# Products of high and low weight parts in the last two feed-forwards: three of 256 columns, or one of 512 and one of 256

## The reference, cut to what matters

```python
def swiglu(x, w_in, w_out):
    gate, up = jnp.split(x @ w_in, 2, axis=-1)
    return (jax.nn.silu(gate) * up) @ w_out
...
for layer in range(DEPTH):
    h = h + 0.5 * rmsnorm(swiglu(rmsnorm(h, g[0]), w_ffn_in[layer, 0], w_ffn_out[layer, 0]), g[1])
    ...  # the mixer, with its own norms
    h = h + 0.5 * rmsnorm(swiglu(rmsnorm(h, g[4]), w_ffn_in[layer, 1], w_ffn_out[layer, 1]), g[5])
```

## Time and profile before

| | |
|---|---|
| median of 3 runs | 1758.89 us (1758.84 to 1761.01) |
| profiled execution | 1760.43 us |
| its span, first to last instruction | 1758.4 us |
| TensorE busy (products) | 1723.0 us, 98% |
| TensorE weight loads busy | 1395.2 us, 79% |
| VectorE busy | 1053.0 us, 60% |
| ScalarE busy | 729.6 us, 41% |
| granted TensorE clock, mean | 0.995 of full |

### The profile page before, as it was taken

One profiled execution on the slowest core, in us unless ns is written; L12 is line 12 of the kernel. 1 busy time (PEld: TensorE's weight loads), 2 busy tenths in 40 slices (PEclk: granted clock), 3 DMA queues, 4 the chain that ended last, 5 costly groups with the idle time before them and its releaser, 6 DMA issues.

```text
span 1758.4 us, 31356 instructions
## 1 busy us (share of the span) xinstructions
PE 1723.0 (98%) x12314; PEld 1395.2 (79%) x12314; DVE 1053.0 (60%) x1905; ACT 729.6 (41%) x1191; POOL 21.2 (1%) x26
## 2 busy tenths in 40 slices
PE   9999999999999999999999999999999999999997
PEld 8999989899999999996899999998953333333332
DVE  7775475787765887578687657866762232222223
ACT  6444463464344544456754446957431101111110
POOL 0000000100000000000000001000020000000000
PEclk9999999999999999999999999999999999999999
DMA  6445334445454355432255545443889999999996
GB/s 243 189 171 193 138 121 161 65 147 191 175 203 149 143 192 203 182 121 95 96 182 200 204 178 193 145 147 119 331 340 428 428 426 428 427 429 428 428 426 258
DMA packets 42342, 409.73 MB, mean 233 GB/s; under 512 B 5304, under 2 KB 5304, under 8 KB 7056
## 3 DMA queue, kind: packets, MB, share of 16 engines
q1 hardware_dynamic: 40032, 402.21, 58.4%
q0 software_dynamic: 1936, 5.79, 1.6%
q10 hardware_dynamic: 288, 0.52, 0.1%
HBM read 405.87 MB, written 2.63 MB: 232 GB/s over the span
## 4 chain that ended last, share of the span: by engine, by line
PE 87%; DMA 6%; DVE 4%; ACT 2%; issue 1%; SPq 0%; DVEq 0%; ACTq 0%
PE ps L626 85%; PE ps L630 2%; DMA branch<-w_gate_up 2%; DMA late<-w_gate_up 2%; DMA soon<-w_gate_up 1%; DVE w_lo L1891 1%; DMA raw<-w_units 1%; ACT w_hi L1388 0%; DMA h<-xT 0%; DVE arena L2335 0%; DVE branch L1914 0%; DVE x_lo L1948 0%; DVE branch L1927 0%; DVE arena L2361 0%; DVE h L1938 0%
## 5 line engine op out<-in xcount | busy, mean ns | idle before, releaser
L626 PE MATMUL ps<-x_hi,w_hi 128*128 128x256 f32 (+1 forms) x2080 | 596.8, 287 | 3.9 <-DVE x_lo L1948 1.8
L626 PE MATMUL ps<-x_lo,w_hi 128*128 128x256 f32 (+1 forms) x2080 | 592.0, 285 | 0.0
L626 PE MATMUL ps<-x_hi,w_lo 128*128 128x256 f32 (+1 forms) x2080 | 590.4, 284 | 0.0
L1891 DVE TENSOR_TENSOR w_lo<-raw,w_hi 128x1024 fp32r<-128x1024 f32 (+1 forms) x352 | 448.2, 1293 | 129.8 <-ACT w_hi L1388 129.0
L1388 ACT ACTIVATE w_hi<-raw 128x1024 fp32r<-128x1024 f32 (+1 forms) x352 | 385.5, 1113 | 184.6 <-PE ps L626 102.1
L626 PEld LDWEIGHTS ps<-x_hi,w_hi 128*128 128x128 f32 x2080 | 391.2, 188 | 10.9 <-issue 6.9
L626 PEld LDWEIGHTS ps<-x_hi,w_lo 128*128 128x128 f32 x2080 | 393.1, 189 | 0.0
L626 PEld LDWEIGHTS ps<-x_lo,w_hi 128*128 128x128 f32 x2080 | 392.1, 189 | 0.3
L626 PE MATMUL ps<-hid_hi,w_hi 128*128 128x272 f32 (+1 forms) x704 | 200.9, 285 | 0.0
L626 PE MATMUL ps<-hid_hi,w_lo 128*128 128x272 f32 (+1 forms) x704 | 200.0, 284 | 0.0
L626 PE MATMUL ps<-hid_lo,w_hi 128*128 128x272 f32 (+1 forms) x704 | 199.4, 283 | 0.0
(11 more groups left out here) (345 smaller groups left out, 2095.4 us busy)
## 6 DMA issues: line engine op xcount, KB each, us to landing
raw<-w_units SPq DMA_DIRECT2D x144, 1024.0 KB, 4.8
soon<-w_gate_up SPq DMA_DIRECT2D x32, 2048.0 KB, 21.8
late<-w_gate_up SPq DMA_DIRECT2D x24, 2048.0 KB, 21.1
raw<-w_out_units SPq DMA_DIRECT2D x32, 1408.0 KB, 6.0
soon<-w_down SPq DMA_DIRECT2D x16, 2048.0 KB, 24.8
late<-w_down SPq DMA_DIRECT2D x12, 2048.0 KB, 22.2
branch<-w_gate_up SPq DMA_DIRECT2D x8, 2048.0 KB, 22.8
branch<-w_down SPq DMA_DIRECT2D x4, 2048.0 KB, 20.4
```

What stands on the lines that cost most here:

```text
L626: return nc.tensor.matmul(out_ap, lhsT, rhs, start=start, stop=stop, skip_group_check=True)
L1891: v.tensor_tensor(part(w_lo, c, 0, n), raw_slot(u, j * n, n), part(w_hi, c, 0, n).bitcast(F32), ALU.subtract).then_inc(lo_made, 1)
```

## The change

In feed-forwards 2 and 3, for units 2 to 21 inward and the first seven tiles outward, the products with the weights' high part become one: the high and low parts of the activations lie in one buffer with two planes (`x_both`, `hid_both`), and one product of 512 columns reads both and writes both halves of a bank. The product with the weights' low part adds into the first half. The two halves have to be added afterwards. Inward, ScalarE copies the second half to SBUF (`halves_copied`), VectorE adds the first half from PSUM, which frees the bank, and then scales (`halves_scaled`); the up tile's copy stands behind the gate's Silu on ScalarE. Outward, ScalarE copies the second half (`out_copied`), VectorE adds the first and frees the bank, and ScalarE squares and scales the sum (`out_scaled`). Buffer sizes don't change. Feed-forwards 0 and 1, units 0 and 1, the last outward tile and all other sections keep the three products.

```diff
+        x_both = sb("x_both", [P, 2, KT * TA], F32R)
+        x_hi, x_lo = x_both[:, 0, :], x_both[:, 1, :]
...
+        def pairs_before(n, it, j):
+            return 2 * ((FT - 2) * (n - 2) + j - 2) + 4 * it
...
+            def in_halves(bank, hi, lo, moving, start, stop):
+
+                first = mm(bank[:, 0:2 * SEQ].rearrange("p (a n) -> p a n", a=2), hi, moving, start, False)
+                return first, mm(bank[:, 0:SEQ], lo, moving[:, 0, :], False, stop)
...
+                        if both is not None:
+                            first, m = in_halves(bank, hi, lo, both[:, :, x], k == 0, k == kt - 1)
...
-                        project(u0 + j, T, 2 * j, X, w, it, 2 * RAW)
+                        project(u0 + j, T, 2 * j, X, w, it, 2 * RAW, both=x_both if w == SEQ else None)
...
+                        if w == SEQ and j < KT - 1:
+                            first, m = in_halves(bank, hi, lo, hid_both[:, :, x], k == 0, k == FT - 1)
...
+                    if halves and m < KT - 1:
+                        nc.scalar.activation(z, filled(t)[:, w:2 * w], ACT.Copy).then_inc(out_copied, 1)
+                        act.wait_ge(evac[t[0]], t[1] + 1)
+                        square(8 * (n // 2) + m, z, w)
+                        nc.scalar.activation(z, z, ACT.Copy, scale=gain(g, m, table)).then_inc(out_scaled, 1)
+                        continue
...
+                def gate_of_halves(j, it):
+                    tg, tu = T.at(2 * j, it, 4), T.at(2 * j + 1, it, 4)
+                    act.wait_ge(hw_made, FT * n + 2 * it + j - 1)
+                    act.wait_ge(full[tg[0]], tg[1] + 1)
+                    nc.scalar.activation(tile(sg, j, w), ps[tg[0]][:, w:2 * w], ACT.Copy).then_inc(halves_copied, 1)
+                    act.wait_ge(halves_scaled, pairs_before(n, it, j) + 1)
+                    nc.scalar.activation(tile(sg, j, w), tile(sg, j, w), ACT.Silu).then_inc(gate_silu, 1)
+                    act.wait_ge(hid_made, FT * n + 2 * it + j - 1)
+                    act.wait_ge(full[tu[0]], tu[1] + 1)
+                    nc.scalar.activation(tile(hw, j, w), ps[tu[0]][:, w:2 * w], ACT.Copy).then_inc(halves_copied, 1)
...
+                    if halves and m < KT - 1:
+                        t = T.at(m)
+                        z = tile(zg, m, w)
+                        copied[0] += 1
+                        dve.wait_ge(out_copied, copied[0])
+                        v.tensor_tensor(z, z, ps[t[0]][:, 0:w], ALU.add).then_inc(evac[t[0]], 1)
...
+                    elif w == SEQ and not (isinstance(it, int) and it == 0):
+                        c = pairs_before(n, it, j)
+                        dve.wait_ge(halves_copied, c + 1)
+                        v.tensor_tensor(g, g, ps[tg[0]][:, 0:w], ALU.add).then_inc(evac[tg[0]], 1)
+                        mine(tg)
+                        v.tensor_tensor(g, g, rs[:, 0:w], ALU.mult).then_inc(halves_scaled, 1)
+                        dve.wait_ge(halves_copied, c + 2)
+                        v.tensor_tensor(x, x, ps[tu[0]][:, 0:w], ALU.add).then_inc(evac[tu[0]], 1)
+                        mine(tu)
+                        v.tensor_tensor(x, x, rs[:, 0:w], ALU.mult).then_inc(halves_scaled, 1)
+                        dve.wait_ge(halves_scaled, c + 2)
```

More of the change, by code:

```diff
@@ L153, in two_blocks @@
         h = sb("h", [P, KT * TA])
-        x_hi = sb("x_hi", [P, KT * TA], F32R)
-        x_lo = sb("x_lo", [P, KT * TA], F32R)
+        x_both = sb("x_both", [P, 2, KT * TA], F32R)
+        x_hi, x_lo = x_both[:, 0, :], x_both[:, 1, :]
         branch = sb("branch", [P, (KT + 8) * TA])
@@ L178, in two_blocks @@
             with ExitStack() as ffn_only:
-                hid_hi = ffn_only.enter_context(nc.sbuf_tensor("hid_hi", [P, FT * TA], F32R))
-                hid_lo = ffn_only.enter_context(nc.sbuf_tensor("hid_lo", [P, FT * TA], F32R))
+                hid_both = ffn_only.enter_context(nc.sbuf_tensor("hid_both", [P, 2, FT * TA], F32R))
+                hid_hi, hid_lo = hid_both[:, 0, :], hid_both[:, 1, :]
                 ffn_only.enter_context(nc.sbuf_tensor("shared_keys", [P, 4 * TA], F32))
@@ L332, in two_blocks @@
         squared, sums_made = sem("squared"), sem("sums_made")
+        halves_copied, halves_scaled = sem("halves_copied"), sem("halves_scaled")
+        out_copied, out_scaled = sem("out_copied"), sem("out_scaled")
         route_sums = sem("route_sums")
@@ L670, in project @@
             def project(u, T, i, src, w, it=0, body=0, kt=KT, n_tiles=2, at=0, x_base=None, between=None, within=None,
-                        made=2, begun=0, done=0):
+                        made=2, begun=0, done=0, both=None):
                 if x_base is not None and n_tiles == 2:
@@ L688, in project @@
                             within()
-                        first, m = three(bank[:, 0:w], part(w_hi, c, a, P), part(w_lo, c, a, P),
-                                         src[0][:, x], src[1][:, x], k == 0, k == kt - 1)
+                        hi, lo = part(w_hi, c, a, P), part(w_lo, c, a, P)
+                        if both is not None:
+                            first, m = in_halves(bank, hi, lo, both[:, :, x], k == 0, k == kt - 1)
+                        else:
+                            first, m = three(bank[:, 0:w], hi, lo, src[0][:, x], src[1][:, x], k == 0, k == kt - 1)
                         if j % (n_tiles // 2) == 0 and k == 0:
@@ L779, in ffn @@
                         x = slice(k * TA, k * TA + w)
-                        first, m = three(bank[:, 0:w], part(w_hi, c, a, P), part(w_lo, c, a, P),
-                                         hid_hi[:, x], hid_lo[:, x], k == 0, k == FT - 1)
+                        hi, lo = part(w_hi, c, a, P), part(w_lo, c, a, P)
+                        if w == SEQ and j < KT - 1:
+                            first, m = in_halves(bank, hi, lo, hid_both[:, :, x], k == 0, k == FT - 1)
+                        else:
+                            first, m = three(bank[:, 0:w], hi, lo, hid_hi[:, x], hid_lo[:, x], k == 0, k == FT - 1)
                         if k % (FT // 2) == 0:
@@ L1447, in root_stat, with branch_out @@
                     nc.scalar.activation(std[:, 0:w], bank[:, 0:w], ACT.Sqrt, scale=1.0 / D).then_inc(evac[t[0]], 1)
-            def branch_out(name, n, g, table, w, per=2):
+            def branch_out(name, n, g, table, w, per=2, halves=False):
                 u0, T = plan[name]
@@ L1457, in branch_out @@
                     t = T.at(m)
+                    z = tile(zg, m, w)
[5 more added lines that the diff above has]
+                        continue
                     bank = filled(t)
                     square(8 * (n // 2) + m, bank[:, 0:w], w)
-                    nc.scalar.activation(tile(zg, m, w), bank[:, 0:w], ACT.Copy,
-                                         scale=gain(g, m, table)).then_inc(evac[t[0]], 1)
+                    nc.scalar.activation(z, bank[:, 0:w], ACT.Copy, scale=gain(g, m, table)).then_inc(evac[t[0]], 1)
                 root_stat(n, w)
@@ L1488, in gate @@
                     nc.scalar.activation(tile(sg, j, w), tile(sg, j, w), ACT.Silu).then_inc(gate_silu, 1)
+                def gate_of_halves(j, it):
[8 more added lines that the diff above has]
+                    nc.scalar.activation(tile(hw, j, w), ps[tu[0]][:, w:2 * w], ACT.Copy).then_inc(halves_copied, 1)
+                later_gate = gate_of_halves if w == SEQ else gate
                 if root is not None:
@@ L1501, in ffn @@
                             split_half(u0 + j + 2, 0, it)
-                            gate(j, it)
+                            later_gate(j, it)
                             split_half(u0 + j + 2, 1, it)
@@ L1507, in ffn @@
                 for j in range(2):
-                    gate(j, FT // 2 - 1)
+                    later_gate(j, FT // 2 - 1)
                     split_to(u0 + FT + j)
-                branch_out(f"out{n}", 2 * G_INDEX[n] + 1, g, halfg, w, 1)
+                branch_out(f"out{n}", 2 * G_INDEX[n] + 1, g, halfg, w, 1, w == SEQ)
             nc.scalar.preload_act_table(ACT.Square)
@@ L1861, in _ @@
         def _(dve):
-            chain, ahead, stds, highs, sums, turns = [0], [0], [0], [0], [0], [0]
+            chain, ahead, stds, highs, sums, turns, copied = [0], [0], [0], [0], [0], [0], [0]
             v = nc.vector
@@ L1973, in residual @@
                 u0, T = plan[name]
+                halves = per == 1 and w == SEQ
                 for m in range(KT):
                     split_to(u0 + m // per + 1, 2 if per == 1 else 2 + m % 2)
+                    if halves and m < KT - 1:
+                        t = T.at(m)
+                        z = tile(zg, m, w)
+                        copied[0] += 1
+                        dve.wait_ge(out_copied, copied[0])
+                        v.tensor_tensor(z, z, ps[t[0]][:, 0:w], ALU.add).then_inc(evac[t[0]], 1)
                     if m < KT - 1:
@@ L1988, in residual @@
                     mine(plan[f"stat{n}"].at(0))
```

(2 more changed lines are left out.)

## The result

The changed kernel takes 1791.92 us in the median (1789.86 to 1793.26, 4 runs) against 1759.72 (4 runs): ratio 1.0178, 95% interval 1.0166 to 1.0189, so 29 to 33 us slower. The forecast was 1791.5. The two profiled executions took 1760.43 and 1789.86 us, 29.4 apart, their spans 1758.4 and 1787.9.

What follows compares the result with a forecast made beforehand. TensorE was taken to bound the last two feed-forwards before, VectorE inward after the change. +35.7 us inward and -3.1 outward gave +32.6, 1793.0 us by the profile and 1791.5 against the median, range 1777 to 1809.

Steps and rivals of the forecast that it cites:

- The bound before: In the last two feed-forwards TensorE sets the pace, busy the whole 113.1 us; VectorE has about a fifth to spare.
- The unit of 6.43 us: Inward: VectorE's time for one changed unit, bounds 6.1 to 6.8, against 5.49 us of TensorE work.
- The sum inward, +35.7: Inward, both feed-forwards: TensorE starts its outward parts late by 19.8 and 15.9 us, +35.7 us.
- The outward sum, -3.1: Outward: 154 steps a feed-forward, each 10.2 ns shorter, 1.6 us twice, -3.1 us; ends 0 and -10.3.
- the 11.2 ns: TensorE's fixed part for each product whatever its width, beyond 106.7 ns for 256 columns at 2.4 GHz.
- The lower end, nothing saved: TensorE's step: the wide product costs as much as two halves made as two products, so nothing is saved.
- Rival (a): Inward: VectorE keeps up and TensorE is the bound again, 5.49 us a unit; with full gain 1749 us; chance 0.04.
- Rival (b): Inward: the weights' landing becomes the bound, 6.25 us a unit; with the longest landing 6.9, 1808 us; chance 0.12.
- Rival (d): Inward: TensorE's clock falls to 1.2 GHz from pausing each unit, a unit 10.8 us, +206 us; chance 0.02.
- The range: Whole kernel: 1777 to 1809 us, from 1779 to 1805 by the unit's bounds, widened by outward ends and the landing.
- the 7 us of the outward ends: Outward: what the ends of the gain there add to the range below; 3 us above.
- my 10.2: TensorE: ns saved by each changed step, 343.4 instead of 353.6, from taking the wide product at 225.5 ns.

Runs made afterwards that it cites:

- out_only: The changed kernel with only the outward part changed; inward keeps three products and the old evacuation: 1758.32 us, ratio 0.9994 to the kernel before.
- first_half: The changed kernel with wide products everywhere, but inward only the first half of the bank is read, with the old evacuation: 1756.51 us, ratio 0.9980.
- splits_first: The changed kernel with both second halves copied before Silu, both tiles added before scaling, and both weight splits ahead of the hidden part: 1758.44 us.
- in_only: The changed kernel with only the inward part changed; outward stays as before: 1792.31 us, ratio 1.0177 to the kernel before.
- chain_only: The changed kernel with each wide product made as two of 256 columns, keeping the new evacuation: 1794.58 us, ratio 1.0186 to the kernel before.
- early_up: The changed kernel with ScalarE copying the up tile's second half before Silu instead of behind it: 1768.25 us, ratio 1.0045 to the kernel before.

## Why the prediction was right

The direction, the place and the size came out by the mechanism forecast: VectorE's unit over TensorE's. Step by step:
- **The bound before**: right. out_only and first_half have TensorE busy throughout the stretch from 588 to 700 us.
- **The unit of 6.43 us**: 6.27 measured. The dependent step in the loop is 0.45 for the scalings (0.54 taken; only hid_lo has 0.56), the up addition comes at 1.63 instead of 1.74, the next split at 3.99 instead of 4.15. The step before hid_hi was 0.65 as taken. The splits' 2.28, for which no row was named, was met as well (661.95 - 659.67). The size was off by 2.5%, inside the bounds of 6.1 and 6.8.
- **The sum inward, +35.7**: from VectorE's first changed unit to outward, 120.2 and 117.5 us against 103.9 and 104.1, so +16.3 and +13.4. 34 periods of 0.16 us less are 5.4 of the 6.0 us missing. Another 0.45 arose ahead of the first unit (597.30 against 596.85); out_only, whose inward part is that of before, has 597.33 too, so it isn't the new evacuation's.
- **The outward sum, -3.1**: -0.6. This term was mis-sized: I took a product with 64 weight columns for one with 128 and two planes. Measured 233.9 ns, forecast 225.5. The experiments explain 4 ns of that by the planes or the weight columns; the other 4 stay open. Nor are the 11.2 ns the same whatever the width, as the prediction has it: 20.6 at 512 columns. The lower end, nothing saved, was the better guess.
- Together 35.7 - 3.1 = 32.6 forecast against 29.5 by the traces: two errors of opposite sign. The median of all runs lies 32.2 above, closer to the forecast than the steps deserve, and that is luck; the profiled run was the fastest of the four.
- **Rival (a)** is what splits_first shows: with another order VectorE keeps up. As the change stands, it doesn't.
- **Rival (b)** was the next bound, as computed, and came out as soon as the chain was shortened. That its 6.25 us stands 0.02 from the measured 6.27 is luck again: from split to split it is 7.40 us (653.41 to 660.81), not 7.2, and the work behind it 5.14 (660.81 to 665.95), not 5.29. Half of the sum is 6.27, so the two bounds were level. A kernel with the chain as it is and the slots freed sooner wasn't run; by the 0.3 us above it would hardly have gained.
- **Rival (d)**: the clock didn't fall inward, but it did once after it (below). Its 10.8 us a unit need the fixed parts too; 16 steps of 640 ns are 10.2.
- **The range**: 1779 less the 7 us of the outward ends is 1772, where the range starts at 1777; the result is far from either.
- The forecast that TensorE would be busy 85% inward was too low, 90 and 93%; its modelled ends may cover part of each wait.

On the two rules weighed. The Trainium skill, "TensorE: Matmul & The Clock Gate", "Back-to-back issue gap", has the gap of columns / 2.4 + 2.5 ns, and calls it that of an isolated product. Worked out from it, as an estimate, a step saves 2.5 ns; 1.8 outward and 5 inward were measured, closer than my 10.2. The height of the gap isn't seen here: 117.9 and 230 to 233.9 ns were measured, against estimates of 109.2 and 215.8 by the formula.

The Trainium skill, "VectorE: DVE Perf Modes", "The DRAIN you can't avoid", measures that a semaphore after each of eight copies costs nothing. That agrees with the 0.33 us between the additions and scalings of splits_first, which signal semaphores too but don't wait for their neighbour. It doesn't carry over to an operation that waits for the one just before it: 0.45 us in the changed kernel's unit.

## What to carry to other kernels

Before a product is made cheaper, write out the period of every engine that evacuates it, with each hand-over, not the busy share: VectorE was about 80% busy here and had no room, because two added operations brought four ordered hand-overs with them. When a chain over two in-order engines is the bound, move the instruction that others wait for ahead of the one that waits (one copy: 24 of 32 us), and set independent operations between dependent ones (0.24 us a unit on VectorE here). Then look at once for the loop just behind, here the raw slots' landing, for it stood level with the first.

## What the runs showed of the hardware

A product of 512 columns saves far less here than a fixed part counted per product would. Outward, beyond its columns at 2.4 GHz, one of 256 columns costs 11.2 ns; one of 512 costs 20.6 reading two planes, and 17 side by side or with 64 weight columns.

TensorE's clock fell for a moment after the pause that ends an inward part. Granted clock (the number after the engines) from 0.5 us after the start of the first outward part, and around and after the start of the second (1028.89), of the changed kernel:

```profile
718.00:722.00 4.00, 4.00 (x17) 3.49 (x16) 3.14 (x7) 2.29 (x4) 0.00 (x0) 0.62 0.50 149
...
1027.00:1031.00 4.00, 2.11 (x12) 1.88 (x13) 3.97 (x5) 0.84 (x2) 0.00 (x0) 1.00 0.36 152
1031.00:1035.00 4.00, 4.00 (x25) 3.51 (x24) 3.14 (x7) 3.88 (x5) 0.00 (x0) 1.00 0.89 324
```

0.62 is a mean of the two levels, 1.2 and 2.4 GHz: mostly 1.2 in the first, 2.4 throughout the second. Both follow a wait of 2.2 us and an inward part with a pause in each unit, and here only the first lost it. The first outward tile took 1.5 us longer than the same tile of feed-forward 3 (727.02 - 717.50 against 1036.89 - 1028.89). in_only and chain_only have the same two waits and lost the clock after all four; their first tiles took 9.45 to 9.60 us. In in_only:

```profile
718.00:722.00 4.00, 4.00 (x23) 4.00 (x22) 3.11 (x8) 2.44 (x4) 0.00 (x0) 0.57 0.52 158
```

After early_up's waits of 1.2 and 1.1 us the clock stayed, and the tile took 8.00. So the changed kernel's profiled execution lost 1.5 us to this and those of in_only and chain_only about 3; what decides it isn't shown. The mean clocks of the changed kernel's four runs, 0.994 to 0.992, fall only roughly as their times rise; whether this makes their spread of 3.4 us wasn't tried.
